# Attentions of block 2: TensorE's step takes the values of four steps back ahead of the turning of two steps back

## The chip, the cores and the metric

The kernel runs on one core of one Trainium2 chip. The metric is the device time of one execution in microseconds, median of several runs. The core's engines are named as the profile names them: PE (TensorE, matmuls), PEld (its weight loads), DVE (VectorE), ACT (ScalarE), POOL (GpSimd), SP (the engine that issues most DMAs).

## The reference

Two transformer blocks of depth 2 follow one another on 512 positions of width 1024, all in float32. The change touches only the two attentions of the second block.

```python
def attend(q, k, v, bias=None, mask=None, sink=None):
    s = jnp.einsum('...qngd,...knd->...ngqk', q, k).astype(jnp.float32) * (HEAD_DIM ** -0.5)
    if bias is not None:
        s = s + bias.astype(jnp.float32)
    if mask is not None:
        s = jnp.where(mask, s, NEG_INF)
...
    p = jax.nn.softmax(s, axis=-1)
...
    return jnp.einsum('...ngqk,...knd->...qngd', p.astype(v.dtype), v)
```

Layer 0 is a neighbourhood attention: 16 heads of 64; the 512 positions are an 8 by 64 grid, a block of 16 grid columns (128 queries) sees a window of 32 grid columns (256 keys) and all 256 context keys, with a learned bias and a mask on the window. The 256 context positions attend to the context keys alone. Layer 1 is a sliding-window attention: 16 query heads on 4 key heads, a block of 128 queries sees the positions within 128 of it and the 256 context keys, with one sink logit for each head in the softmax.

## The kernel before

Activations lie transposed in SBUF (features on the 128 partitions), so a tile of 128 features holds two heads of 64, one in each half of the partitions. Every engine has a program of its own, written out by hand in the order in which it runs; semaphores alone tie them together. No scheduler moves anything.

Both attentions are software pipelines over steps. A step `s` is one block of 128 queries of one tile (two heads). In the neighbourhood attention (`na`) a tile has 6 steps, `j, b = divmod(s, 6)`: b = 0 to 3 are the four latent blocks (scores 512 wide), b = 4 and 5 the two context blocks (256 wide); 8 tiles give 48 steps. In the sliding-window attention (`swa`) a tile has 4 steps, `tile, b = divmod(s, 4)`: b = 0 and 3 are 512 wide, b = 1 and 2 are 640 wide; 8 tiles give 32 steps. One step's data passes these stations:

- PE `score(s)` (L984 in `na`, L1068 in `swa`): queries times keys for the two heads into PSUM. `na` has two sets of PSUM banks for it and waits for the bias of two steps back; `swa` has one and waits for the bias of the step before.
- DVE `bias(s)` (L1926, L1988): adds the bias or band, with the row's minimum on the side, and writes `n_s` or `s_s` in SBUF (three buffers).
- ACT `exp(s)` (L1431, L1471): exponential with row sums, in place.
- DVE `probs(s)` (L1932 and L1935, L1995 and L1998): reciprocal and scaling. DVE runs `bias(s)` and then `probs(s-1)` in its step s.
- PE `turn(s)` (L1005, L1082): transposes the probabilities, 128 by 128 at a time, into PSUM banks of which there is one set. It waits for `probs(s)` and for `keep(s-1)`.
- ACT `keep(s)` (L1440, L1479): copies the turned probabilities to `n_pT` or `s_pT` in SBUF (two buffers). It waits for `values(s-2)`. ACT runs `exp(s)` and then `keep(s-2)` in its step s.
- PE `values(s)` (L1023, L1094): turned probabilities times values, into bank 2 or 3 of PSUM. It waits for `keep(s)`.
- DVE `take_latent`, `take_context` (L1940, L1945) and `take_out` (L2003): copy a finished tile's result out. The first `values` of a later tile waits for them.

`turn_v` (L996) is 9 extra transposes for each tile of `na`, which turn the values of the next tile; they stand at the end of the PE steps with b = 4, 5 and 0, and ACT copies them (`keep_v`, L1424). POOL builds the bias tables of the next tile of `na` meanwhile (L557), from strips that SP fetches.

In the kernel before, step s of PE is `score(s)`, `turn(s-2)`, `values(s-3)`, `turn_v`.

Of the kernel before, what the change touches and what calls it, by code (L numbers as in the profile page):

```python
# [228 lines left out]
def build(nc, d, out):  # L229
# [3 lines left out]
    with ExitStack() as stack:  # L233
# [141 lines left out]
        def bank(i, n=512):  # L375
            return ps[:, 512 * i:512 * i + n]
# [264 lines left out]
        def _(pe):  # L641
# [327 lines left out]
            def na(ph):  # L969

                def score(s):
                    j, b = divmod(s, 6)
                    if s >= 2:
                        pe.wait_ge(n_biased, 2 * (s - 1))
                    last = [None, None]
                    if b < 4:
                        window = slice(KEY_COL[b] * ROWS, KEY_COL[b] * ROWS + 2 * P)
                        parts = ((slice(b * P, b * P + P), window, 0), (slice(b * P, b * P + P), slice(S, T2), 2 * P))
                    else:
                        parts = ((slice(S + (b - 4) * P, S + (b - 3) * P), slice(S, T2), 0),)  # L980
                    for queries, keys, to in parts:
                        for hd in range(2):
                            half = slice(HD * hd, HD * hd + HD)
                            last[hd] = pe.matmul(bank(4 + 2 * (s % 2) + hd)[:, to:to + 2 * P], proj[half, j, queries],  # L984
                                                 proj[half, 8 + j, keys], start=True, stop=True)
                    for hd in range(2):
                        last[hd].then_inc(n_scored, 1)

                def turn_v(j, part):
                    if part:  # L990
                        pe.wait_ge(n_v_kept, 3 * j + part)
                    elif j >= 2:
                        pe.wait_ge(n_taken, 2 * (j - 1))
                    for t in range(4 * part, min(4 * part + 4, 9)):
                        frm = 8 * ROWS * t if t < 7 else S + (t - 7) * P
                        last = pe.transpose(bank(3)[:, t % 4 * P:t % 4 * P + P], proj[:, 16 + j, frm:frm + P], mat(IDENT))  # L996
                    last.then_inc(n_v_turned, 1)

                def turn(s):
                    pe.wait_ge(n_probs, 2 * s + 2)  # L1000
                    if s:
                        pe.wait_ge(n_kept, s)
                    for hd in range(2):
                        for c in range(4 if s % 6 < 4 else 2):
                            last = pe.transpose(bank(hd)[:, c * P:c * P + P], n_s[s % 3][:, hd, c * P:c * P + P],  # L1005
                                                mat(IDENT))
                    last.then_inc(n_turned, 1)

                def values(s):
                    j, b = divmod(s, 6)  # L1010
                    pe.wait_ge(n_kept, s + 1)
                    if b == 0:
                        pe.wait_ge(n_v_kept, 3 * j + 3)
                    if b == 4 and j < 7:
                        pe.wait_ge(n_v_kept, 3 * j + 6)
                    if j and b in (0, 4):
                        pe.wait_ge(n_taken, 2 * j - (b == 0))
                    to, tiles = (bank(2)[:, b * P:b * P + P], [KEY_COL[b] // 8, KEY_COL[b] // 8 + 2, 7, 8]) if b < 4 else \
                        (bank(3)[:, (b - 4) * P:(b - 3) * P], [7, 8])
                    for c, v in enumerate(tiles):  # L1020
                        for hd in range(2):
                            half = slice(HD * hd, HD * hd + HD)
                            last = pe.matmul(to[half, :], n_vs[j % 2][:, v, half], n_pT[s % 2][:, hd, c * P:c * P + P],  # L1023
                                             start=(c == 0), stop=(c == len(tiles) - 1))
                            if c == len(tiles) - 1:
                                last.then_inc(n_values, 1)

                pe.wait_ge(acc_free, ph["unit0"])
                for s in range(48 + 3):
                    j, b = divmod(s, 6)  # L1030
                    if s < 48:
                        score(s)
                    if j == 0 and b < 3:
                        turn_v(0, b)
                    if 2 <= s < 50:
                        turn(s - 2)
                    if s >= 3:
                        values(s - 3)
                    if s >= 4 and (s - 4) % 6 < 3 and (s + 2) // 6 < 8:
                        turn_v((s + 2) // 6, (s - 4) % 6)  # L1040

            def swa(ph):
                pe.wait_ge(acc_free, ph["unit0"])
                pe.wait_ge(hn_out, ph["hn0"])
                for n in range(len(ROPE_AT), ROPE_TILES):
                    rotate(ph, n)
                    kv = n - len(ROPE_AT)
                    if kv < 2:
                        for t in range(6):
                            last = pe.transpose(ps[:, 2 * S * kv + t * P:2 * S * kv + t * P + P],  # L1050
                                                proj[:, 10 + kv, t * P:t * P + P], mat(IDENT))
                        last.then_inc(s_v_turned, 1)
                pe.wait_ge(rope_a, ROPE_TILES)
                pe.wait_ge(rope_out, ROPE_TILES)

                def score(s):
                    tile, b = divmod(s, 4)
                    if s:
                        pe.wait_ge(s_biased, 2 * s)
                    lo, hi = max(b - 1, 0) * P, min(b + 2, 4) * P  # L1060
                    n = hi - lo
                    parts = ((lo, hi, 0), (S, T2, n)) if n == 2 * P else \
                        ((lo, hi, 0), (S, S + P, n), (S + P, T2, n + P))
                    last = [None, None]
                    for frm, end, to in parts:
                        for hd in range(2):
                            half = slice(HD * hd, HD * hd + HD)
                            last[hd] = pe.matmul(sums[hd][:, to:to + end - frm], proj[half, tile, b * P:b * P + P],  # L1068
                                                 proj[half, 8 + tile // 4, frm:end], start=True, stop=True)
                    for hd in range(2):  # L1070
                        last[hd].then_inc(s_scored, 1)

                def turn(s):
                    pe.wait_ge(s_probs, 2 * s + 2)
                    if s:
                        pe.wait_ge(s_kept, s)
                    else:
                        pe.wait_ge(s_v_kept, 2)
                    for hd in range(2):
                        for c in range(5 if 0 < s % 4 < 3 else 4):  # L1080
                            at_ = (5 * hd + c) * P
                            last = pe.transpose(ps[:, at_:at_ + P], s_s[s % 3][:, hd, c * P:c * P + P], mat(IDENT))  # L1082
                    last.then_inc(s_turned, 1)

                def values(s):
                    tile, b = divmod(s, 4)
                    pe.wait_ge(s_kept, s + 1)
                    if tile and b == 0:
                        pe.wait_ge(s_taken, tile)
                    tiles = list(range(max(b - 1, 0), min(b + 2, 4))) + [4, 5]  # L1090
                    for c, v in enumerate(tiles):
                        for hd in range(2):
                            half = slice(HD * hd, HD * hd + HD)
                            last = pe.matmul(bank(3)[half, b * P:b * P + P], s_vs[tile // 4][:, v, half],  # L1094
                                             s_pT[s % 2][:, hd, c * P:c * P + P],
                                             start=(c == 0), stop=(c == len(tiles) - 1))
                            if c == len(tiles) - 1:
                                last.then_inc(s_values, 1)

                for s in range(32 + 3):  # L1100
                    if s < 32:
                        score(s)
                    if 2 <= s < 34:
                        turn(s - 2)
                    if s >= 3:
                        values(s - 3)

            pe.wait_ge(mats_in, 16)
            for ph in phases:
# [1075 lines left out]
```

## Time and profile before

| | us |
|---|---|
| median of 3 runs | 3113.66 (3112.57 to 3115.39) |
| profiled execution, its time | 3117.72 |
| profiled execution, its span | 3115.9 |
| of it, neighbourhood attention | about 1637 to 1796 |
| of it, sliding-window attention | about 2560 to 2690 |
| PE busy over the span | 3005.2 (96%) |
| DVE, ACT, POOL busy over the span | 1598.7, 1147.8, 1093.1 |
| mean granted TensorE clock | 0.983 |

PE bounds the whole kernel, and most of it is one matmul behind the other in the projections. The two attentions together are 290 us of the span; in them PE waits for DVE and ACT at many steps, and these waits are short. The table of shares doesn't show that: the stages have to be opened one by one.

### The profile page before, as it was taken

To read this page: it belongs to the slowest core of one execution; us is meant where nothing else is said; L and a number is where in the kernel's file an instruction comes from. 1 tells how busy PE (TensorE), PEld (TensorE's weight loads), DVE (VectorE), ACT (ScalarE), POOL (GpSimd) and SP (SyncE) were. 2 spreads that over 40 slices of the span, in tenths; PEclk is the share of its full clock that TensorE was granted. 3 is DMA by queue.
4 is the path that set the end of the run, shared out by engine and by line. 5 is a ranking of instruction groups with operands and counts; after the bars stand their busy time and mean duration, and the time that the engine had idled before them with its cause. 6 is when DMAs were issued, how large, how long until landed. Compare 5 with 4: busy or idle time off the path is not lost.

```text
span 3115.9 us, 46695 instructions
## 1 busy us (share of the span) xinstructions
PE 3005.2 (96%) x16904; PEld 2405.0 (77%) x16904; DVE 1598.7 (51%) x2539; ACT 1147.8 (37%) x1756; POOL 1093.1 (35%) x506
## 2 busy tenths in 40 slices
PE   8999999999999999999998999999999999999999
PEld 6866788876857788877786678888888667778887
DVE  4457654555357554554317746541553347567272
ACT  3364442222264542232217733321232227533232
POOL 3433444443433444442232132222223330244443
PEclk9999999998999999999999999999999899999999
DMA  4421343442411343431110011121111110022223
GB/s 162 138 103 40 124 153 123 142 140 89 162 59 61 128 141 129 148 115 48 57 54 27 25 48 54 61 69 54 66 66 63 61 55 1 33 83 98 91 94 101
DMA packets 72795, 269.97 MB, mean 87 GB/s; under 512 B 7920, under 2 KB 8944, under 8 KB 72560
## 3 DMA queue, kind: packets, MB, share of 16 engines
q1 hardware_dynamic: 71024, 264.34, 25.4%
q10 hardware_dynamic: 1664, 4.18, 0.4%
q8 instruction: 70, 1.15, 0.2%
q14 instruction: 37, 0.30, 0.0%
HBM read 266.39 MB, written 2.10 MB: 86 GB/s over the span
## 4 chain that ended last, share of the span: by engine, by line
PE 56%; issue 27%; POOL 8%; DVE 6%; ACT 2%; DMA 1%; POOLq 0%; ACTq 0%; SPq 0%; DVEq 0%
PE ps L665 42%; POOL w_lo L542 7%; PE ps L692 4%; PE ps L738 1%; DVE s_s L1998 1%; PE ps L838 1%; PE ps L849 1%; PE ps L1005 1%; PE ps L1023 1%; PE ps L984 1%; DVE s_s L1988 1%; PE ps L873 1%; PE ps L830 1%; DVE n_s L1935 1%; DMA w_raw<-w_in_dram 1%
## 5 line engine op out<-in xcount | busy, mean ns | idle before, releaser
L542 POOL TENSOR_TENSOR w_lo<-w_raw,w_hi 128x1024 fp32r<-128x1024 f32 (+1 forms) x364 | 945.7, 2599 | 1526.0 <-ACT w_hi L1142 1526.0
L665 PE MATMUL ps<-h_hi,w_hi 128*128 128x512 f32 (+1 forms) x2832 | 957.7, 372 | 3.4 <-POOL w_lo L542 1.7
L665 PE MATMUL ps<-h_lo,w_hi 128*128 128x512 f32 (+1 forms) x2832 | 946.8, 368 | 0.0
L665 PE MATMUL ps<-h_hi,w_lo 128*128 128x512 f32 (+1 forms) x2832 | 945.4, 368 | 0.0
L1142 ACT ACTIVATE w_hi<-w_raw 128x1024 fp32r<-128x1024 f32 (+1 forms) x364 | 406.4, 1117 | 1369.0 <-PE ps L665 1219.1
L665 PEld LDWEIGHTS ps<-h_hi,w_hi 128*128 128x128 f32 x2832 | 491.2, 188 | 109.4 <-issue 7.3
L665 PEld LDWEIGHTS ps<-h_lo,w_hi 128*128 128x128 f32 x2832 | 491.9, 188 | 90.1
L665 PEld LDWEIGHTS ps<-h_hi,w_lo 128*128 128x128 f32 x2832 | 490.5, 188 | 91.7
L1778 DVE TENSOR_SCALAR conv_y<-u_pad,small 128x770 f32<-128x770 f32 (+1 forms) x88 | 175.8, 1997 | 196.1 <-ACT u_pad L1323 195.6
L1576 DVE CUSTOM_DVE_ANT_0 mod_junk<-mod_w,silu_c 128x1024 f32<-128x1024 f32 x96 | 138.4, 1442 | 127.1 <-DMA mod_w<-w_mod_dram 126.5
L1731 DVE SCALAR_TENSOR_TENSOR xT<-ps,mod,xT 128x512 f32 (+1 forms) x72 | 45.5, 659 | 304.4 <-PE ps L665 259.0
L1781 DVE SCALAR_TENSOR_TENSOR conv_y<-u_pad,small,conv_y 128x770 f32<-128x770 f32 (+1 forms) x176 | 156.1, 887 | 24.4 <-DVE conv_y L1781 6.7
L1579 DVE CUSTOM_DVE_ANT_0 mod_junk<-mod_w,silu_c 128x1024 f32<-128x1024 f32 x96 | 152.9, 1593 | 3.3
L1755 DVE TENSOR_TENSOR glu_a<-ps,glu_g 128x512 f32<-128x512 f32 x44 | 30.5, 692 | 188.6 <-PE ps L665 181.9
L1757 DVE TENSOR_TENSOR b_lo<-glu_a,b_hi 128x512 f32 x44 | 105.5, 2397 | 41.6 <-ACT b_hi L1304 41.6
L665 PE MATMUL ps<-a_hi,w_hi 128*128 128x512 f32 (+1 forms) x396 | 119.9, 357 | 1.5 <-POOL w_lo L542 1.5
L665 PE MATMUL ps<-a_lo,w_hi 128*128 128x512 f32 (+1 forms) x396 | 120.0, 357 | 0.0
L665 PE MATMUL ps<-a_hi,w_lo 128*128 128x512 f32 (+1 forms) x396 | 120.0, 357 | 0.0
L665 PE MATMUL ps<-b_hi,w_hi 128*128 128x512 f32 x264 | 104.8, 397 | 2.8 <-POOL w_lo L542 2.8
L665 PE MATMUL ps<-b_hi,w_lo 128*128 128x512 f32 x264 | 104.4, 395 | 0.0
L665 PE MATMUL ps<-b_lo,w_hi 128*128 128x512 f32 x264 | 104.4, 395 | 0.0
L1731 DVE SCALAR_TENSOR_TENSOR xT<-ps,xT 128x512 f32 (+1 forms) x48 | 33.2, 691 | 130.9 <-PE ps L665 104.9
(212 smaller groups left out, 3792.7 us busy)
## 6 DMA issues: line engine op xcount, KB each, us to landing
mod_w<-w_mod_dram SPq DMA_DIRECT2D x96, 512.0 KB, 3.4
w_raw<-w_gu_dram SPq DMA_DIRECT2D x88, 512.0 KB, 3.3
w_raw<-w_down_dram SPq DMA_DIRECT2D x64, 704.0 KB, 4.0
w_raw<-w_up_dram SPq DMA_DIRECT2D x88, 512.0 KB, 3.3
w_raw<-w_in_dram SPq DMA_DIRECT2D x56, 512.0 KB, 3.4
w_raw<-na_qkv_dram SPq DMA_DIRECT2D x24, 512.0 KB, 3.2
w_raw<-w_out_dram SPq DMA_DIRECT2D x16, 512.0 KB, 3.3
w_raw<-swa_qkv_dram SPq DMA_DIRECT2D x12, 512.0 KB, 3.3
```

Of the source, the lines that this page charges most:

```text
L542: pool.tensor_tensor(w_lo[par][:, 0:cols], w_raw[par][:, 0:cols], w_hi[par][:, 0:cols].bitcast(F32), ALU.subtract).then_inc(w_lo_ready, 1)
L665: last = pe.matmul(acc[par][:, to:to + n], w[par][:, k * P:k * P + P], r[:, k, frm:frm + n], start=begin, stop=end)
L692: last = pe.matmul(acc[par][:, to:to + n], w[par][:, k * P:k * P + P], r[:, k, frm:frm + n], start=begin, stop=end)
L738: return [pe.matmul(sums[0][:, to:to + w], mats[g // 2 * HD:g // 2 * HD + HD, SPREAD64 + g % 2, :], r[g // 2 * HD:g // 2 * HD + HD, frm:fr ...
L830: pe.matmul(bank(hd), proj1[half, 12 + j, b * P:b * P + P], proj1[half, 8 + j, :], start=True, stop=True).then_inc(x_scored, 1)
L1142: act.activation(w_hi[par][:, 0:K * P], w_raw[par][:, 0:K * P], ACT.Copy).then_inc(w_hi_ready, 1)
L1576: dve.tensor_tensor_reduce(mod_junk[:], mod_w[:], silu_c[:, 0, :], 1.0, 0.0, ALU.mult, ALU.add, mod_sum[:, 0:1]).then_inc(mod_step, 1)
L1579: dve.tensor_tensor_reduce(mod_junk[:], mod_w[:], silu_c[:, 1, :], 1.0, 0.0, ALU.mult, ALU.add, mod_sum[:, 1:2]).then_inc(mod_step, 1)
L1731: last = dve.scalar_tensor_tensor(out=x_, in0=row(acc[par][:, to:to + n]), scalar=gate, in1=x_, op0=ALU.mult, op1=ALU.add)
L1757: dve.tensor_tensor(b_lo[:, bass.ds(f, 1), :], row(glu_a[:]), b_hi[:, bass.ds(f, 1), :].bitcast(F32), ALU.subtract).then_inc(a_lo_ready, 1)
L1778: dve.tensor_scalar(y, u, tap(0), tap(3), ALU.mult, ALU.add).then_inc(conv_step, 1)
L1781: dve.scalar_tensor_tensor(out=y, in0=u, scalar=tap(j), in1=y, op0=ALU.mult, op1=ALU.add).then_inc(conv_step, 1)
```

## The change

In both attentions PE's step s becomes `score(s)`, `values(s-4)`, `turn(s-2)`, `turn_v`: the values come ahead of the turning, and they are those of one step further back. The loop has one more step to finish. No instruction is added or taken away (PE has the same number of instructions), and the programs of DVE, ACT, POOL and SP are the same as before, as are all buffers and all waits.

```diff
@@ na @@
-                for s in range(48 + 3):
+                for s in range(48 + 4):
                     j, b = divmod(s, 6)
                     if s < 48:
                         score(s)
                     if j == 0 and b < 3:
                         turn_v(0, b)
+                    if s >= 4:
+                        values(s - 4)
                     if 2 <= s < 50:
                         turn(s - 2)
-                    if s >= 3:
-                        values(s - 3)
                     if s >= 4 and (s - 4) % 6 < 3 and (s + 2) // 6 < 8:
                         turn_v((s + 2) // 6, (s - 4) % 6)
@@ swa @@
-                for s in range(32 + 3):
+                for s in range(32 + 4):
                     if s < 32:
                         score(s)
+                    if s >= 4:
+                        values(s - 4)
                     if 2 <= s < 34:
                         turn(s - 2)
-                    if s >= 3:
-                        values(s - 3)
```

On PE in the neighbourhood attention, the end of step b = 4, step b = 5 and step b = 0 of a tile. `n_s_132` to `n_s_134` are the three buffers of probabilities (L1005 is `turn`), `n_pT_135` and `n_pT_136` the two of turned probabilities (L1023 is `values`), `proj_77` in L984 is `score` and in L996 `turn_v`. Before:

```order
L1005 MATMUL ps<-mats_59,n_s_134 128x128 x8
L1023 MATMUL ps<-n_pT_136,n_vs_130 64x128 x8
L996 MATMUL ps<-mats_59,proj_77 128x128 x4
L984 MATMUL ps<-proj_77 128x256 x2
L1005 MATMUL ps<-mats_59,n_s_132 128x128 x8
L1023 MATMUL ps<-n_pT_135,n_vs_130 64x128 x8
L996 MATMUL ps<-mats_59,proj_77 128x128 x4
L984 MATMUL ps<-proj_77 128x256 x4
```

The same place in the changed kernel:

```order
L1005 MATMUL ps<-mats_59,n_s_134 128x128 x8
L996 MATMUL ps<-mats_59,proj_77 128x128 x4
L984 MATMUL ps<-proj_77 128x256 x2
L1023 MATMUL ps<-n_pT_136,n_vs_130 64x128 x8
L1005 MATMUL ps<-mats_59,n_s_132 128x128 x8
L996 MATMUL ps<-mats_59,proj_77 128x128 x4
L984 MATMUL ps<-proj_77 128x256 x4
L1023 MATMUL ps<-n_pT_135,n_vs_130 64x128 x8
```

The values that stood between a turning and the next score now stand behind that score.

On PE in the sliding-window attention, from the turning in a step b = 2 on; `s_s` are probabilities (L1082), `s_pT` turned ones (L1094), L1068 is `score`. Before:

```order
L1082 MATMUL ps<-mats_59,s_s_142 128x128 x8
L1094 MATMUL ps<-s_pT_145,s_vs_140 64x128 x10
L1068 MATMUL ps<-proj_77 128x384 x2
L1068 MATMUL ps<-proj_77 128x128 x4
L1082 MATMUL ps<-mats_59,s_s_143 128x128 x8
L1094 MATMUL ps<-s_pT_146,s_vs_140 64x128 x8
L1068 MATMUL ps<-proj_77 128x256 x4
```

The same place in the changed kernel:

```order
L1082 MATMUL ps<-mats_59,s_s_142 128x128 x8
L1068 MATMUL ps<-proj_77 128x384 x2
L1068 MATMUL ps<-proj_77 128x128 x4
L1094 MATMUL ps<-s_pT_145,s_vs_140 64x128 x10
L1082 MATMUL ps<-mats_59,s_s_143 128x128 x8
L1068 MATMUL ps<-proj_77 128x256 x4
L1094 MATMUL ps<-s_pT_146,s_vs_140 64x128 x8
```

Here too a turning is followed directly by the next score, and each group of values stands between that score and the next turning.

## Rows read from the trace of the kernel before

**Rows 1.** Windows of the two stages: length, busy PE, PEld, DVE, ACT, POOL; clock.

```profile
1636.00:1797.00 161.00, 142.10 (x1352) 102.79 (x1352) 119.78 (x400) 117.77 (x271) 34.82 (x44) 1.00 0.08 25
2531.00:2692.00 161.00, 141.67 (x1305) 107.96 (x1304) 112.89 (x320) 93.71 (x173) 17.57 (x13) 0.96 0.04 13
```

**Rows 2.** Waits in the neighbourhood attention: us in total, times, longest.

```profile
PEld ps L1023 <- issue: 7.9, 47, 0.2
PE ps L1005 <- DVE n_s L1935: 11.7, 26, 0.7
...
DVE pace L1922 <- issue: 17.5, 9, 2.3
DVE n_s L1926 <- issue: 14.2, 9, 1.8
```

**Rows 3.** Waits of PE in the sliding-window attention, window 2575 to 2682.

```profile
PE ps L1082 <- ACT s_pT L1479: 4.5, 14, 0.4
PE ps L1094 <- DVE proj L2003: 4.0, 7, 0.6
```

**Rows 4.** Timeline, neighbourhood attention, steps b = 4, 5, 0: start, duration, what, [idle before].

```profile
1688.97 1.09 PE L1005 MATMUL ps<-mats,n_s 128*128 128x128 f32 x8 [0.44 <-DVE n_s L1935]
...
1689.99 1.09 PE L1023 MATMUL ps<-n_pT,n_vs 128*64 128x128 f32 x16
...
1691.02 0.66 PE L996 MATMUL ps<-mats,proj 128*128 128x128 f32 x4
1691.60 0.70 PE L984 MATMUL ps<-proj 64*128 64x256 f32 x4
...
1692.24 1.09 PE L1005 MATMUL ps<-mats,n_s 128*128 128x128 f32 x8
1692.39 0.42 DVE L1926 CUSTOM_DVE_ANT_0 n_s<-ps,n_bias 128x256 f32<-128x256 f32 x1 [1.78 <-issue]
...
1694.87 1.13 PE L984 MATMUL ps<-proj 64*128 64x256 f32 x8
...
1696.16 0.06 DVE L1922 MEMSET pace<- 128x1 f32 x1 [2.27 <-issue]
```

**Rows 5.** The same timeline at the next step b = 4.

```profile
1707.35 1.00 ACT L1440 ACTIVATE n_pT<-ps 128x1024 f32<-128x1024 f32 x1
...
1708.38 0.41 DVE L1926 CUSTOM_DVE_ANT_0 n_s<-ps,n_bias 128x256 f32<-128x256 f32 x1
...
1708.51 1.09 PE L1005 MATMUL ps<-mats,n_s 128*128 128x128 f32 x8 [0.44 <-DVE n_s L1935]
```

**Rows 6.** Timeline, sliding-window attention, one tile from b = 3 to b = 3.

```profile
2603.61 0.75 DVE L1988 CUSTOM_DVE_ANT_0 s_s<-ps,s_band,small 128x512 f32<-128x512 f32 x1 [0.49 <-issue]
...
2603.93 1.28 PE L1082 MATMUL ps<-mats,s_s 128*128 128x128 f32 x10 [0.40 <-ACT s_pT L1479]
...
2605.78 1.09 PE L1094 MATMUL ps<-s_pT,s_vs 128*64 128x128 f32 x16 [0.57 <-DVE proj L2003]
...
2606.81 1.13 PE L1068 MATMUL ps<-proj 64*128 64x256 f32 x8
2607.87 1.31 PE L1082 MATMUL ps<-mats,s_s 128*128 128x128 f32 x10
...
2609.11 1.31 PE L1094 MATMUL ps<-s_pT,s_vs 128*64 128x128 f32 x20
...
2610.36 1.36 PE L1068 MATMUL ps<-proj 64*128 64x384 f32 x12
...
2611.80 0.88 DVE L1988 CUSTOM_DVE_ANT_0 s_s<-ps,s_band,small 128x640 f32<-128x640 f32 x1 [1.27 <-issue]
...
2614.36 1.00 ACT L1479 ACTIVATE s_pT<-ps 128x1024 f32<-128x1024 f32 x1
...
2615.50 1.07 PE L1082 MATMUL ps<-mats,s_s 128*128 128x128 f32 x8 [0.23 <-ACT s_pT L1479]
...
2618.74 0.75 DVE L1988 CUSTOM_DVE_ANT_0 s_s<-ps,s_band,small 128x512 f32<-128x512 f32 x1 [0.49 <-issue]
```

## The prediction, made before the changed kernel was run

> **What bounds the kernel now.** I read the windows of the two stages first: PE is busy 142 of 161 us in each, DVE 120 and 113, ACT 118 and 94 [rows 1]. So PE is the fullest engine, but in neither stage full, and what it could gain there is at most its gaps. The granted clock is 1.00 (the 2.4 GHz level) in the first window and 0.96 in the second, which takes in the slow start of that stage; nothing in the steady steps is explained by the clock. Next come the waits. In the neighbourhood attention PE waits 26 times in front of a turning for DVE's scaling, and DVE is idle in two places only, 9 times each, for 31.7 us in all: about once in every tile in front of the bias of step b = 5 and once in front of that of b = 0 [rows 2]. In the sliding-window attention PE waits in front of turnings for ACT's copy of turned probabilities and, once in a tile, in front of the values for the taking of the tile before [rows 3]. Last the timelines of one tile of each, which give a chain that closes on itself.
>
> **How a tile of the neighbourhood attention runs.** The time from the start of one PE group to the start of the next is what the group costs PE. Read as differences of starts: a turning of 8 transposes costs 1.02 (1688.97 to 1689.99), the values 1.03, a `turn_v` of four 0.58, a narrow score 0.64, the turning, values and `turn_v` of step 5 together 2.63, a wide score 1.06 (the wide one is taken from the sliding-window stage, 2606.81 to 2607.87) [rows 4, 6]. DVE's bias starts 0.15 behind the end of a narrow score, and about 0.23 behind that of a wide one; the turning of step 4 starts 0.13 behind DVE's start of that step. From step b = 0 to the next b = 4 DVE never waits: it goes from 1696.16 to 1708.38, 12.22 us without a wait [rows 4, 5], which the two idle places of rows 2 confirm. So the tile's cycle is: 0.13, then on PE turning 1.02, values 1.03, `turn_v` 0.58, score 0.64, turning 1.02, values 1.03, `turn_v` 0.58, score 1.06, then 0.23 and DVE's 12.22. The sum is 19.54; the trace has 1708.51 - 1688.97 = 19.54 [rows 4, 5]. PE sets the time from b = 4 to b = 0, DVE the rest.
>
> **Part 1, the neighbourhood attention.** In the new order the values of step 4 stand ahead of the turning that waits 0.44 for DVE. They are ready, since their copy was waited for by an earlier turning. Of the cycle above one of the two groups of values, 1.03, drops out: behind DVE's release PE goes turning, `turn_v`, score, (values, turning), `turn_v`, score. The second group stays, as PE is behind there and has no wait to put it in. For this the values must be done before DVE releases the turning of step 4. They are: between the turning of step b = 3 and that of b = 4 PE has the same three groups in either order (turning, values, narrow score), and in the old one they are done in time for a wait of 0.44 [rows 4, 5]. ACT's copy in front of it ends at 1708.35, 0.16 ahead of the turning at 1708.51 [rows 5], and hangs on DVE, not on the values. The new cycle is 18.5 us, 1.03 less, in 8 tiles: 8.2 us. The last tile has no `turn_v` and no POOL beside it; its chain of turnings, values and score is the same, so I take the same term there.
>
> What is late next: DVE from b = 0 to b = 4, so that moving the values in those steps brings nothing; only 1 of 6 steps pays. Nothing is added to a queue: SP's fetches and POOL's tables hang on DVE's bias and come 1 us earlier each tile with it.
>
> **Part 2, the sliding-window attention.** A tile takes 2618.74 - 2603.61 = 15.13 us [rows 6]. PE's groups, as differences of starts: scores 1.06 (b = 0, 3) and 1.29 (b = 1, 2: 2610.36 to the bias at 2611.80, less 0.15); turnings 1.24 (x10: b = 1, 2) and 1.02 (x8); values 1.03 (x16: b = 0, 3) and 1.25 (x20: b = 1, 2) [rows 4, 6]. Twice each: 4.70 + 4.52 + 4.56 = 13.78. The difference, 1.35, is PE's waits: 0.40 and 0.23 for ACT's copies, 0.57 for the taking, each with the short hole that the sequence leaves around it [rows 6].
>
> In the new order each of the three is covered. (a) ACT's copy in step b = 1 ends at 2615.36, 3.56 behind that step's bias at 2611.80, and the next turning can start 3.70 behind it [rows 6]. With values of 1.03 or 1.25 between score and turning, PE reaches it at turning + score + values = 3.3 to 3.8 behind the turning before, and walking through the four steps of a tile PE arrives 0.5 to 1.1 us after the copy. (b) The first values of a tile now stand in the next step, about 1.0 us behind the end of the taking. (c) The single score buffer is the new risk, since a score now comes directly behind a turning. The bias of b = 2 starts 0.15 behind its score's end; PE has values 1.25 and a turning 1.02 to do and reaches score b = 3 at 2.12 behind the bias's start. The bias is two passes of 0.88, and with 0.1 for the passing on it is over after about 1.8. That leaves 0.3, the tightest place. So PE should not wait at all, and the tile takes 13.78: 1.35 less. Between the bias of the first b = 3 and that of the last lie 7 tiles: 9.5 us. The first steps run at the lower clock and have no values yet, and the last turnings and values hang on ACT's copies one by one, so the ends get nothing (0 to 0.5).
>
> **The unknown cost, the new neighbours.** A group of values directly behind a score occurs nowhere in the trace; before, all values follow a turning. From rows: 16 values cost 1.03 and 8 turnings 1.02 whatever follows, a score of the same work 1.06, so a follower of a score costs 0.04 more than one of another group [rows 4, 6]. I take 0: one group follows a score in either order. Bounds: the loader idles 0.17 in front of nearly every group of values [rows 2]; if that hole vanishes or doubles behind a score, the sliding-window stage changes by 32 x 0.17 = 5.4 us and the PE part of the other (2 of 6 steps, 16 in all) by 2.7, together 8.1 us either way.
>
> The Trainium skill ("TensorE: Matmul & The Clock Gate", section "Step-by-step: what each phase is for") says that a weight load runs ahead of matmuls in flight when its row group doesn't conflict or it goes to the background buffer. By its first condition the loads of the values (all rows) conflict with a score (half the rows) as those of a turning do, and the sum stays 17.7; by its second the hole of 0.17 should not be there at all, and the gain could be up to the 8.1 us larger. The loader's wait in rows 2, 47 times, speaks for the first.
>
> **Sum.** 8.2 + 9.5 = 17.7 us. The profiled execution would go from 3117.7 to 3100.0; it lies 4.1 above the median of the runs, and that difference stays. For the median: 3113.7 - 17.7 = 3096.0.
>
> **Rivals.**
> (1) *Only one stage gains.* In the neighbourhood stage it may be that ACT's copy, which is only 0.16 ahead of the turning now, holds it; then 3113.7 - 9.5 = 3104.2. In the other the score buffer or the copy may take the place of the waits, since each margin there is under half a microsecond at its tightest; then 3105.5. For it: the margins. Against: the chains above reproduce the old cycle to 0.02 us.
> (2) *The waits only move.* PE waits in front of the turning for as long as before plus the values' time, and the gain is gone: 3113.7. For it: DVE sets 4 of 6 steps. Against: DVE idles 31.7 us in the stage [rows 2], and it idles for PE.
> (3) *Slower: the turning is what is urgent.* In the steps where PE is behind (b = 5, 0, 1 of each tile, 24 in all) the turning starts one group of values later. ACT's copy follows it, and the next exponential stands behind that copy in ACT's queue. If this chain were critical it would cost 24 x 1.03 = 24.7 against 17.7: 3120.7. It decides from where the copy ends later than the next bias's first half; a turning 1.02, a copy 1.00 and two passings of about 0.1 make 2.2 us, and the next turning comes 2.9 us or more later. So 0.7 us is left, and the trace speaks against it.
> (4) *More gain*, by the loads of the values pulled under the score: 3096.0 - 8.1 = 3087.9.
> That the change doesn't do what it says can be left out: the order on PE shows it.
>
> **Chances.** Forecast 0.68 (own range 3092 to 3100, small errors of neighbours and ends), rival 1 0.14, rival 2 0.08, rival 3 0.04, rival 4 0.06. From 3091 to 3107 lie the forecast and rival 1, with a part of rival 4: above 8 in 10. Faster by over 0.2% (6.2 us, about what a measurement can tell from no change) are the forecast and rivals 1 and 4: 0.88. Same 0.08, slower 0.04.
>
> **What the profile of the changed kernel would show.** A tile of the neighbourhood attention from turning to turning in 18.5 instead of 19.54; DVE's idle time in front of b = 5 falls from 1.78 to about 0.75, that in front of b = 0 stays at 2.3. The sliding-window tile in 13.8 instead of 15.1, with no wait for L2003 and none for L1479 in the steady tiles. It would be wrong if PE's values behind a score start later than 0.2 us behind the score's other followers, if DVE or ACT waits appear in front of L984 or L1068, or if the cycle stays at 19.5 or 15.1.

## The result, and the profile after

The changed kernel takes 3098.44 us, the median of 4 runs (3094.91 to 3103.38), against 3114.52 for the kernel before (4 runs, 3112.57 to 3119.8). The ratio is 0.9947, with a 95% interval of 0.9931 to 0.9963. Measured again beside the experiments it took 3096.06 (6 runs, 3094.19 to 3098.2) against 3113.85, ratio 0.9943 (0.9931 to 0.9955). So it is faster by 16 to 18 us; 17.7, and a median of 3096.0, had been forecast.

First the windows of the two stages, to set beside [rows 1]. Columns: start and end, length, busy PE, PEld, DVE, ACT, POOL, clock, DMA share, GB/s. After:

```profile
1638.40:1787.10 148.70, 138.38 (x1352) 102.84 (x1352) 119.73 (x400) 114.43 (x267) 34.82 (x43) 1.00 0.09 27
2557.10:2681.10 124.00, 117.78 (x1188) 92.43 (x1189) 94.54 (x299) 90.82 (x170) 5.02 (x5) 0.94 0.02 6
```

The same two stretches, cut at like places, in the kernel before:

```profile
1637.10:1796.10 159.00, 142.10 (x1352) 102.79 (x1352) 119.78 (x400) 115.89 (x268) 34.82 (x43) 1.00 0.08 25
2562.20:2695.40 133.20, 118.05 (x1187) 92.18 (x1188) 94.60 (x298) 90.57 (x170) 5.06 (x4) 0.95 0.02 5
```

The stages are 10.3 and 9.2 us shorter. DVE is as busy as before to a tenth of a microsecond, and PE in the second stage to 0.3: what went is idle time. In the first stage PE's busy time fell as well, by 3.7 us with the same 1352 matmuls, which the prediction had not foreseen. About 3 us of it are transposes that now stand next to transposes (see e6).

The waits of the changed kernel in the neighbourhood attention, window 1640 to 1787 (total, times, longest), answer to [rows 2]:

```profile
DVE pace L1922 <- PE ps L984: 16.0, 9, 2.1
PEld ps L1023 <- issue: 12.8, 40, 0.3
...
PE ps L1005 <- DVE n_s L1935: 5.6, 13, 0.4
...
DVE n_s L1926 <- issue: 4.3, 7, 0.6
```

DVE's wait in front of step b = 5 fell from 1.8 to 0.6, and the one in front of b = 0 is still there, 2.1 instead of 2.3. PE waits for DVE's scaling 13 times instead of 26. In the sliding-window attention no wait of PE for L1479 or L2003, the two of [rows 3], is left in the window 2570 to 2668. One wait of 0.3 us for DVE's bias stands there, in front of the score at 2570.75, where the stage comes out of the low clock.

The timeline of one tile of the neighbourhood attention, steps b = 4, 5, 0 and the next b = 4 (start, duration, what, [idle before]), answers to [rows 4, 5]:

```profile
1687.63 1.09 PE L1005 MATMUL ps<-mats,n_s 128*128 128x128 f32 x8 [0.44 <-DVE n_s L1935]
...
1688.56 0.60 PE L996 MATMUL ps<-mats,proj 128*128 128x128 f32 x4
...
1689.09 0.70 PE L984 MATMUL ps<-proj 64*128 64x256 f32 x4
1689.72 1.09 PE L1023 MATMUL ps<-n_pT,n_vs 128*64 128x128 f32 x16
...
1689.87 0.42 DVE L1926 CUSTOM_DVE_ANT_0 n_s<-ps,n_bias 128x256 f32<-128x256 f32 x1 [0.61 <-issue]
...
1690.74 1.09 PE L1005 MATMUL ps<-mats,n_s 128*128 128x128 f32 x8
...
1691.67 0.60 PE L996 MATMUL ps<-mats,proj 128*128 128x128 f32 x4
...
1692.20 1.13 PE L984 MATMUL ps<-proj 64*128 64x256 f32 x8
...
1693.50 0.06 DVE L1922 MEMSET pace<- 128x1 f32 x1 [2.13 <-PE ps L984]
...
1705.72 0.41 DVE L1926 CUSTOM_DVE_ANT_0 n_s<-ps,n_bias 128x256 f32<-128x256 f32 x1
...
1705.85 0.88 PE L1005 MATMUL ps<-mats,n_s 128*128 128x128 f32 x6 [0.44 <-DVE n_s L1935]
```

The tile takes 1705.85 - 1687.63 = 18.22 us (19.54 before, 18.5 forecast). DVE's part, 1693.50 to 1705.72, is 12.22, the very value of before. PE's part is 1693.50 - 1687.63 = 5.87. As differences of starts, turning 0.93, `turn_v` 0.53, score 0.63, values 1.02, turning 0.93, `turn_v` 0.53, and the wide score with what DVE needs behind it 1.30.

One tile of the sliding-window attention after, from b = 1 on, answers to [rows 6]:

```profile
2589.29 0.88 DVE L1988 CUSTOM_DVE_ANT_0 s_s<-ps,s_band,small 128x640 f32<-128x640 f32 x1 [1.06 <-issue]
...
2592.70 1.31 PE L1094 MATMUL ps<-s_pT,s_vs 128*64 128x128 f32 x20
2592.85 0.88 DVE L1988 CUSTOM_DVE_ANT_0 s_s<-ps,s_band,small 128x640 f32<-128x640 f32 x1 [0.79 <-issue]
...
2593.94 1.09 PE L1082 MATMUL ps<-mats,s_s 128*128 128x128 f32 x8
...
2594.97 1.13 PE L1068 MATMUL ps<-proj 64*128 64x256 f32 x8
...
2596.03 1.09 PE L1094 MATMUL ps<-s_pT,s_vs 128*64 128x128 f32 x16
...
2597.05 1.31 PE L1082 MATMUL ps<-mats,s_s 128*128 128x128 f32 x10
...
2597.52 0.69 DVE L2003 COPY proj<-ps 128x512 f32<-128x512 f32 x1
...
2598.30 1.14 PE L1068 MATMUL ps<-proj 64*128 64x256 f32 x8
...
2599.36 1.09 PE L1094 MATMUL ps<-s_pT,s_vs 128*64 128x128 f32 x16
...
2603.07 0.88 DVE L1988 CUSTOM_DVE_ANT_0 s_s<-ps,s_band,small 128x640 f32<-128x640 f32 x1 [1.05 <-issue]
```

From bias to bias 13.78 us, as forecast, and no PE row has an idle time in brackets: in these tiles PE is now the bound.

### The profile page after: what moved, and what is told of

It reads as the page before. It is cut to its first block, busy times and chain, and to the rows that moved or that the text cites. A ratio compares the mean times of both kernels' runs of the same rounds, so it can differ in the third digit from the quotient of the medians.

```text
span 3101.6 us, 46695 instructions
## 1 busy us (share of the span) xinstructions
PE 3004.8 (97%) x16904; PEld 2405.6 (78%) x16904; DVE 1600.4 (52%) x2539; ACT 1146.6 (37%) x1756; POOL 1091.8 (35%) x506
## 4 chain that ended last, share of the span: by engine, by line
PE 56%; issue 26%; POOL 8%; DVE 6%; ACT 2%; DMA 1%; POOLq 0%; ACTq 0%; SPq 0%; DVEq 0%
PE ps L665 43%; POOL w_lo L542 7%; PE ps L692 4%; PE ps L738 1%; PE ps L849 1%; DVE s_s L1998 1%; PE ps L838 1%; DVE n_s L1935 1%; DVE s_s L1988 1%; PE ps L830 1%; PE ps L1005 1%; PE ps L873 1%; PE ps L984 1%; PE ps L752 1%; PE ps L1023 1%
```

## The experiments

All kernels keep the programs of DVE, POOL and SP, and ACT's too but for one run, named there. What differs is the order on PE. The stages' lengths, from the first score's start to the end of the last values in each profile, serve to compare them, since the rest of a span moves by itself (see the last section). Stage 1 is the neighbourhood attention, stage 2 the sliding-window attention. The columns: the tile that repeats in each stage, each stage's length, the end of each stage (from DVE's bias of b = 4, or of b = 3, in the last tile to the end of the last values), and the ratio to before with its interval.

| run | tile 1 | tile 2 | stage 1 | stage 2 | end 1 | end 2 | ratio (95%) |
|---|---|---|---|---|---|---|---|
| before | 19.55 | 15.13 | 158.4 | 128.8 | 9.3 | 9.6 | |
| changed kernel | 18.24 | 13.78 | 148.2 | 119.5 | 9.4 | 9.6 | 0.9947 (0.9931 to 0.9963) |
| e1 only stage 1 | 18.25 | 15.13 | 148.2 | 129.0 | 9.4 | 9.6 | 0.9967 (0.9955 to 0.9979) |
| e2 only stage 2 | 19.55 | 13.78 | 158.4 | 119.5 | 9.3 | 9.6 | 0.9975 (0.9966 to 0.9984) |
| e3 lag alone | 20.56 | 15.49 | 168.5 | 136.4 | 12.6 | 14.7 | 1.0063 (1.0048 to 1.0079) |
| e4 order alone | 19.30 | 16.65 | 159.2 | 145.7 | 11.8 | 14.3 | 1.0064 (1.0049 to 1.0079) |
| e5 one step ahead | 19.63 | 15.13 | 161.1 | 128.8 | 11.6 | 9.6 | 1.0016 (1.0007 to 1.0026) |
| e6 `turn_v` next | 19.27 | 15.13 | 156.2 | 128.9 | 9.3 | 9.6 | 0.9991 (0.9982 to 1.0001) |
| e7 `turn_v` later | 17.93 | 13.77 | 146.7 | 119.3 | 9.3 | 9.6 | 0.9935 (0.9923 to 0.9947) |
| e8 some steps ahead | 18.75 | 14.48 | 153.9 | 127.2 | 10.9 | 12.0 | 0.9980 (0.9970 to 0.9989) |

**e1 and e2: each stage alone.** The change is made in `na` alone, then in `swa` alone.

> Only the neighbourhood attention has the new order, the sliding-window attention the old one. Theory A (one group of values, 1.03 us, leaves the chain of PE between the turning of step b = 4 and the score of b = 0; the transposes that now follow transposes switch faster by a further 0.3 us a tile): a tile takes 18.2 us as in the changed kernel, the time falls by 9 to 10 us. The sliding-window tile stays at 15.1 us. Rival B (the two attentions help each other, or part of the gain is a matter of the clock): the time falls by clearly more or less than that, and the two single gains do not add up to the whole.

> Only the sliding-window attention has the new order. Theory A (PE's waits for ACT's copy and for the taking of a finished tile are covered by values): a tile takes 13.8 us against 15.1, the time falls by 9.3 us. The tile of the neighbourhood attention stays at 19.5 us. Rival B: as for the run before, the gains do not add up.

Measured: 3103.73 and 3106.13 us against 3114.72, so -11.0 and -8.6. The stages' lengths change by -10.2 and -9.3, each as in the full change, and the other stage stays. The two parts are independent, and both are real: the medians add up to 19.6 us, the stages to 19.5. Rival 1 falls.

**e3: the longer lag without the new order.**

```diff
                     if 2 <= s < 50:
                         turn(s - 2)
-                    if s >= 3:
-                        values(s - 3)
+                    if s >= 4:
+                        values(s - 4)
```

and the same in `swa`, with the loops one step longer.

> In both attentions the values are those of four steps back, but behind the turning as in the kernel before: score(s), turn(s-2), values(s-4), turn_v. Theory A (order and lag are both needed): in the neighbourhood attention nothing changes, 19.5 us a tile. In the sliding-window attention the wait for the taking goes, but ACT's copy now waits for the values behind the turning; the loop turning, values, copy gives 3.7 us in two steps and 3.5 in the others, 14.4 us a tile, so some 5 us less for the kernel. Rival C (it is the lag alone that gives the gain): 18.2 and 13.8 us a tile, 16 us less.

Measured: 3133.65 us, 18.9 more. This missed: both stages got slower, by 1.0 and 0.4 us a tile. The trace shows whose wait it is, in step b = 1 and, below, in b = 5 (L1940 is the taking of a tile, L1440 the copy of turned probabilities, L1023 the values):

```profile
1701.19 0.69 DVE L1940 COPY proj<-ps 128x512 f32<-128x512 f32 x1 [0.58 <-PE ps L1023]
...
1711.76 1.02 ACT L1440 ACTIVATE n_pT<-ps 128x1024 f32<-128x1024 f32 x1 [0.82 <-PE ps L1023]
```

Two engines wait in it for values that now stand behind a turning. DVE's taking of a finished tile hangs on the last values of that tile, and DVE's scaling of the next probabilities is queued behind the taking. ACT's copy needs the buffer that the values of four steps back read.

The tiles are less than half of the loss: from the first tile's b = 4 or 3 to the last one's the stages lose 6.9 and 1.8 us. Another 3.3 and 5.1 are lost in the two ends, where no score stands between the last turnings, and PE, DVE and ACT wait for each other in turn. In the sliding-window attention (in the kernel before, ACT's copy at that place had waited 1.46 for its turning):

```profile
2695.09 2.21 PE L1082 MATMUL ps<-mats,s_s 128*128 128x128 f32 x10 [1.95 <-DVE s_s L1998]
...
2699.18 1.24 ACT L1479 ACTIVATE s_pT<-ps 128x1280 f32<-128x1280 f32 x1 [4.67 <-PE ps L1094]
...
2700.56 1.06 PE L1082 MATMUL ps<-mats,s_s 128*128 128x128 f32 x8 [1.52 <-ACT s_pT L1479]
```

A part of these 5.1 us is the clock: the granted clock was 0.66 from 2696 to 2700, after PE had been busy for 2.05 of the 4 us before, and the turning took 2.21 instead of 1.28. That part may differ from execution to execution.

**e4: the new order without the longer lag.** The values of three steps back stand ahead of the turning.

> In both attentions the values come ahead of the turning, but they are those of three steps back as in the kernel before: score(s), values(s-3), turn(s-2), turn_v. Theory A (the values must be ready when PE comes to them): in the neighbourhood attention a tile stays at 19.5 us, since the copy that the values wait for ends when DVE releases the turning. In the sliding-window attention PE waits for the copy and, once a tile, for the taking in front of the values, and the turning comes later by both: some 16.3 us a tile, 8 us more for the kernel. Rival D (the order alone gives the gain): 18.2 and 13.8 us a tile, 16 us less.

Measured: 3132.58 us, 17.9 more, where 8 had been expected. The neighbourhood stage changes by only 0.8 us (its tiles are 0.25 shorter, its end 2.5 longer), the sliding-window stage by 16.9. Four of its tiles take 16.65, near the 16.3 expected; what was missed are the end, 4.7 longer, and two slower tiles (below). A turn of one tile there:

```profile
2639.33 0.69 DVE L2003 COPY proj<-ps 128x512 f32<-128x512 f32 x1
...
2640.16 1.09 PE L1094 MATMUL ps<-s_pT,s_vs 128*64 128x128 f32 x16 [2.26 <-DVE proj L2003]
```

The first values of a tile stand in step b = 3, ahead of the turning, and need the bank that DVE empties in that same step, behind a bias that itself waits for that step's score. PE waits 15.8 us for it in 7 tiles. The lag of four moves those values to the next step, where the taking is over. So neither half of the change shortens a stage alone: the order needs the lag, and the lag needs the order. Here two of the tiles took 18.1 and 18.2 instead of 16.65. In both the granted clock fell for some microseconds, while the other tiles of the same program kept 1.00. The first of them, with PE busy for 3.18 and then 2.54 of 4 us:

```profile
2600.00:2604.00 4.00, 3.18 (x32) 2.40 (x32) 3.58 (x13) 2.64 (x5) 0.00 (x0) 1.00 0.00 0
2604.00:2608.00 4.00, 2.54 (x19) 2.24 (x20) 2.40 (x8) 1.52 (x4) 0.00 (x0) 0.64 0.00 0
```

**e5: values ahead of the turning in step b = 4 alone**, in `na`, behind it in all others, with the lag of four. The prediction had said that only this step pays.

```diff
+                    if s >= 4 and b == 4:
+                        values(s - 4)
                     if 2 <= s < 50:
                         turn(s - 2)
-                    if s >= 3:
-                        values(s - 3)
+                    if s >= 4 and b != 4:
+                        values(s - 4)
```

> Only the neighbourhood attention is changed: values of four steps back in all steps, but ahead of the turning in step b = 4 alone; in the five others they stand behind it as before. Theory A (only b = 4 pays, since DVE sets the pace from b = 0 to b = 4 and PE is behind in b = 5): a tile takes 18.4 us (the full change has 18.2; one of the two cheap switches from turning to the turning of values is lost), 9 us less for the kernel. Rival G (every step's wait gives a share): a tile takes about 19.3 us, a sixth of the gain.

Measured: 3118.14 us against 3113.85, the tile 19.63, the end of the stage 2.3 longer. Missed by 1.2 us a tile. Step b = 4 does what was said (DVE's idle time in front of the bias of b = 5 is 0.61, as in the full change, and the tile is 0.93 shorter than in e3), but the other steps give it back:

```profile
1706.48 0.42 DVE L1947 COPY proj<-ps 128x256 f32<-128x256 f32 x1 [0.58 <-PE ps L1023]
...
1710.60 1.07 PE L1005 MATMUL ps<-mats,n_s 128*128 128x128 f32 x8 [0.32 <-ACT n_pT L1442]
```

**e8: values ahead where a taking hangs on them.** To tell the takings (theory T) from ACT's copies (theory C), the values stand ahead in steps b = 1, 3 and 4 of the neighbourhood attention and in step b = 3 of the other, behind in the rest.

```diff
@@ na, against e5 @@
-                    if s >= 4 and b == 4:
+                    if s >= 4 and b in (1, 3, 4):
                         values(s - 4)
                     if 2 <= s < 50:
                         turn(s - 2)
-                    if s >= 4 and b != 4:
+                    if s >= 4 and b not in (1, 3, 4):
                         values(s - 4)
@@ swa, against the kernel before @@
+                    if s >= 4 and s % 4 == 3:
+                        values(s - 4)
                     if 2 <= s < 34:
                         turn(s - 2)
-                    if s >= 3:
-                        values(s - 3)
+                    if s >= 4 and s % 4 != 3:
+                        values(s - 4)
```

> The values are those of four steps back everywhere, but they stand ahead of the turning only where a taking by DVE or the b = 4 turning hangs on them: in steps b = 1, 3 and 4 of the neighbourhood attention, and in step b = 3 of the sliding-window attention. In all other steps they stand behind the turning. Theory T (the longer lag costs what it does because DVE's takings of a finished tile, which stand ahead of DVE's scalings, wait for values behind a turning): the neighbourhood tile of 19.63 us with values ahead in b = 4 alone loses the two takings' waits of 0.58 and comes to 18.5; the sliding-window tile of 15.49 us with all values behind loses the 1.28 that the taking waited, 14.2. The whole: 8 x 1.04 + 7 x 0.93 = 14.8 us less than before, about 3099. Theory C (what costs is that ACT's copies wait for values that stand behind the turning; the takings' waits are cover for that): the copies still wait in the steps left, so the neighbourhood tile stays at 19.2 or more and the sliding-window tile at 15.1 or more; about 3112 or longer.

Measured: tiles of 18.75 and 14.48, 3109.18 us against 3115.95. The takings bring 0.88 of the 1.16 expected (from e5's 19.63) and 1.01 of the 1.28 (from e3's 15.49), below theory C's floors of 19.2 and 15.1. In the neighbourhood attention only the takings' waits went: ACT's copies wait for values 7 times and 6.3 us in the window 1650 to 1780 of e5 as of e8, and the takings, 13 times and 7.3 us in e5, no longer. There the takings are shown to be the cause. In the sliding-window attention the copy of step b = 3 waited for the same values as the taking (0.45 beside 1.28 in e3), so the run moves both; that the next turning waited 0.88 in e3 for DVE's scaling, which is queued behind the taking, speaks for the taking.

0.5 and 0.7 us are left to the full change's 18.24 and 13.78. PE's waits for copies in the steady tiles of e8, windows 1650 to 1780 and 2570 to 2665:

```profile
PE ps L1005 <- ACT n_pT L1444: 2.5, 8, 0.3
...
PE ps L1084 <- ACT s_pT L1483: 3.7, 13, 0.4
```

In the neighbourhood tile this wait makes 0.39 of the 0.51: score and wait in step b = 5 take 1.02, the score 0.63 in the full change. The other 0.12 come from the turning and `turn_v` of that step, which don't stand side by side (e6). In the other tile two such waits, each with its short hole, make the 0.7.

The whole got 6.1 us shorter by its stages and 6.8 by the medians, less than half of the 14.8 expected: the tiles gave 6.1 and 4.3, and the ends, where the values stand behind the turning, took back 1.6 and 2.5.

**e6: what a neighbour costs.** In the old order, `turn_v` stands between the turning and the values, in `na`.

```diff
                         turn(s - 2)
-                    if s >= 3:
-                        values(s - 3)
                     if s >= 4 and (s - 4) % 6 < 3 and (s + 2) // 6 < 8:
                         turn_v((s + 2) // 6, (s - 4) % 6)
+                    if s >= 3:
+                        values(s - 3)
```

> Only the neighbourhood attention is changed, and neither lag nor order of values and turning: the turning of values (turn_v) stands directly behind the turning and ahead of the values of three steps back. Theory A (the surplus of 0.3 us a tile over the forecast is a faster switch between two groups of transposes, 0.93 against 1.02 us for the group in front): a tile takes 19.3 to 19.4 us against 19.54, 1 to 2 us less for the kernel. Rival H (the surplus has to do with the values' new place): 19.5 us a tile, no change.

Measured: the tile 19.27, and on PE:

```profile
1685.68 1.09 PE L1005 MATMUL ps<-mats,n_s 128*128 128x128 f32 x8 [0.46 <-DVE n_s L1935]
1686.61 0.60 PE L996 MATMUL ps<-mats,proj 128*128 128x128 f32 x4
1687.14 1.09 PE L1023 MATMUL ps<-n_pT,n_vs 128*64 128x128 f32 x16
1688.16 0.70 PE L984 MATMUL ps<-proj 64*128 64x256 f32 x4
1688.79 1.09 PE L1005 MATMUL ps<-mats,n_s 128*128 128x128 f32 x8
```

Turning 0.93 and `turn_v` 0.53, where they cost 1.02 and 0.58 in [rows 4]; the values keep 1.02. Only the two groups of transposes that stand side by side got cheaper, the one in front by 0.09 and the one behind by 0.05. The ratio, 0.9991 (0.9982 to 1.0001), can't be told from no change; the tile can.

**e7: `turn_v` and ACT's copy of it one step later**, on top of the full change. In step b = 4 the score then follows the turning directly.

```diff
-                    if s >= 4 and (s - 4) % 6 < 3 and (s + 2) // 6 < 8:
-                        turn_v((s + 2) // 6, (s - 4) % 6)
+                    if s >= 5 and (s - 5) % 6 < 3 and (s + 1) // 6 < 8:
+                        turn_v((s + 1) // 6, (s - 5) % 6)
```

and the same condition for `keep_v` on ACT.

> The changed kernel with turn_v, and ACT's copies of it, one step later: at the end of the steps b = 5, 0 and 1 in place of 4, 5 and 0. Theory A (the chain of PE from the turning of b = 4 to the score of b = 0 is what a tile is waiting for, and it holds two groups of turn_v): one of them, 0.5 to 0.6 us, leaves the chain and goes where PE waits for DVE; a tile takes 17.7 us against 18.2, some 4 us less than the changed kernel, 20 less than the one before. Rival I (something else is late by then, as ACT's copies): 18.2 us a tile as in the changed kernel.

Measured: 3093.54 us (3091.97 to 3095.29) against 3096.06 for the changed kernel beside it, 2.5 less where 4 had been expected. The two ranges overlap a little; the stage is 1.5 shorter. It is the fastest version here. DVE's idle time in front of b = 5 falls again, as the same mechanism says:

```profile
1701.99 0.42 DVE L1926 CUSTOM_DVE_ANT_0 n_s<-ps,n_bias 128x256 f32<-128x256 f32 x1 [0.17 <-issue]
...
1711.77 0.66 PE L1023 MATMUL ps<-n_pT,n_vs 128*64 128x128 f32 x8 [0.41 <-ACT n_pT L1440]
```

The tile is 17.93, not 17.7, for two reasons. With no transposes behind it the turning of b = 4 costs 1.02 again, so PE's part from there to DVE's start of b = 0 is 5.44 against 5.87, 0.43 less and not 0.53. And step b = 1 now holds a full `turn_v` instead of a short one, so PE is the pace from b = 0 to b = 1 (turning, `turn_v`, score and values, 3.11 us together): from DVE's bias of b = 0 to that of b = 1 it is 3.11 instead of 2.99.

**The changed kernel again**, for the unchanged stretches.

> The changed kernel once more, unaltered, to have a second profile of it on another occasion. Both theories on the tiles: 18.22 and 13.78 us a tile again, to 0.05. Theory E (the 1.3 to 4 us by which unchanged stretches differ between the first two profiles are the moments at which the granted clock rises and falls, which differ from execution to execution): the stretches between landmarks outside the attentions differ again by 1 us or more from the first profile, and with them the total. Rival F (the new order itself makes PE find a lower clock at the start of the projection behind the neighbourhood attention, 0.77 and 0.89 in the first 10 us of it against 1.00 before): the same low values stand there again.

Measured: the attentions take 148.2 and 119.3, as in the first profile to 0.2, and its span is 3092.8 instead of 3101.6. Behind the last tile of the neighbourhood attention the first profile had a low clock, this one the full one:

```profile
1788.00:1793.00 5.00, 4.01 (x15) 3.30 (x16) 4.26 (x2) 5.00 (x7) 4.95 (x3) 0.77 0.00 0
1793.00:1798.00 5.00, 5.00 (x27) 4.29 (x27) 5.00 (x3) 1.61 (x3) 4.40 (x2) 0.89 0.00 0
```

and the second profile at that place:

```profile
1785.00:1790.00 5.00, 3.90 (x19) 2.96 (x20) 4.29 (x2) 5.00 (x7) 4.98 (x3) 1.00 0.00 0
1790.00:1795.00 5.00, 5.00 (x30) 4.35 (x29) 5.00 (x3) 1.58 (x3) 4.39 (x2) 1.00 0.00 0
```

So the low clock there is one execution's, not the change's. Over the whole spans the mean granted clock is 0.983 in the first profile and 0.986 in the second.

## Why the prediction was right

**The mechanism of part 1 held, its size was under-estimated.** DVE's chain of 12.22 us stayed to the hundredth, and the wait in front of b = 5 fell to 0.61 (0.75 forecast). The tile lost 1.31 instead of 1.03. The mis-sized term is the sum of PE's groups: the rows of before gave a turning 1.02 and a `turn_v` 0.58, because values stood between them. In the new order the two stand side by side, and they cost 0.93 and 0.53. Twice (0.09 + 0.05) = 0.28 is the whole surplus. e6 confirms it with another order. The term "8 x 1.03 = 8.2" has two more errors that nearly cancel: 6 tiles repeat, not 8, and the last one gained 2.50 (19.23 to 16.73), not 1.03. Together 6 x 1.31 + 2.50 = 10.4, against 10.2 measured by the stage.

**Why the last tile gains more.** The prediction took "the same term" for a tile without POOL beside it. Without POOL, DVE is no longer the pace there. DVE's scaling (L1935) in one step of a steady tile of the changed kernel, and in the like step of the last tile:

```profile
1700.77 1.84 DVE L1935 TENSOR_SCALAR n_s<-n_s,stats 128x512 f32<-128x512 f32 x2
...
1773.50 0.88 DVE L1935 TENSOR_SCALAR n_s<-n_s,stats 128x512 f32<-128x512 f32 x2
```

While POOL builds its tables the scaling takes 1.51 to 1.84, else 0.88. From b = 0 to b = 4 DVE needs 12.22 in a steady tile of either kernel; in the last tile it took 11.90 before (1774.36 to 1786.26) and takes 10.74 after (1766.43 to 1777.17), and these 1.16 are nearly all of what the last tile gains beyond 1.31. There the loop through PE and ACT sets the pace of several steps, and the values drop out of it more than once: in the kernel before, the bias of b = 2 started at 1780.16 and that of b = 3 at 1783.24, 3.08 apart, with PE's turning waiting 0.42 for ACT's copy; after, 1772.08 and 1774.61, 2.53 apart. The Trainium skill ("Perfetto Trace Analysis", section "Optimizing Scalar/DVE Operations") says that GpSimd and DVE share an SBUF read port; the trace fits that, with 1.84 against 0.88.

**"Only 1 of 6 steps pays"** held in the steady tiles as to what the order gains over the old one, and fails as a recipe: e5 shows that the other steps need the new order too, to pay for the longer lag. The prediction priced the lag at nothing. That was right only because the order comes with it, and it had not said so. e3 puts the price of the lag alone at 18.9 us, of which 8.7 lie in the tiles and 8.4 in the ends of the stages, in part at a low clock; in the full change the ends are as before to 0.2.

**Part 2 held in every step.** 13.78 was forecast and measured. The margins: (a) the copy of b = 1 ends at 2592.86, the turning starts at 2593.94, 1.08 behind it; (b) the taking ends at 2598.21, the values start at 2599.36; (c) the tight one, the second bias of b = 2 ends at 2594.54 (2593.66 + 0.88) and the next score starts at 2594.97, 0.43 behind it, where 0.3 was forecast. Seven tiles by 1.35 are 9.5; the stage lost 9.3.

**The new neighbour cost nothing**, as taken. A narrow score followed by values costs 0.63 (0.64 before), a wide one 1.06 (2594.97 to 2596.03). The loader's hole in front of the values is what changed, from 0.2 at most to 0.3, in 40 places; the matmuls' starts don't show it. The bound had been made from that hole, and it was not a cost at all. So rival 4 and the second condition of the page cited there ("TensorE: Matmul & The Clock Gate" of the Trainium skill, section "Step-by-step: what each phase is for") get no support: the hole didn't vanish, it grew, and the values' price stayed.

**The sum.** The stages gave 10.2 + 9.3 = 19.5, against 17.7. By medians it was 16.1 the first time and 17.8 the second. The 1.8 of surplus lies within what the unchanged stretches vary by, so that a median falls on the forecast to 0.1 is luck; what was right is each part and its size to within 2 us. Rival 2 (the waits only move) falls with DVE's idle time of b = 5, rival 3 (the turning is urgent) with the tiles: its margin of 0.7 us sufficed. The waits that it is built from exist, though, once the values stand on the wrong side of the turning, as e3 shows for ACT's copy.

## What to carry to other kernels

Put the work that nobody waits for in front of the instruction that waits, and check both of its ends: what frees its inputs, and which engine is queued behind something that needs its output. A lag and an order that are each a loss alone can be a gain together, so undo them one at a time before judging either. Read a group's cost as the difference of starts for the neighbour that it will have, since the same eight transposes cost 1.02 or 0.93 by what follows. Look at the ends of the stages too: in four of these runs a few microseconds were lost there that no steady tile shows.

## What the runs showed of the hardware

- Eight transposes of 128 x 128 (f32) cost 1.02 us when values or a score follow and 0.93 when four more transposes do. Those four cost 0.53 behind the eight, whether values or a score follow them, and 0.58 behind values or a score. Sixteen matmuls of values cost 1.02 to 1.03 whatever stands around them.
- DVE's scaling of 2 x 128x512 takes 0.88 us, and 1.51 to 1.84 while POOL adds its tables.
- In stretches whose program is the same, executions differ. From the end of the last values of the neighbourhood attention to the first score of the sliding-window attention it took 759.7 to 768.5 us in eleven profiles, and 768.5 and 763.4 in two of one kernel. Between these two the clock differs (0.77 and 0.89 against 1.00 over 10 us, above). For the eleven it isn't the whole cause: e1, with the highest mean clock (0.988), took 764.9, and e5, with 0.986, 759.7. Differences of a few microseconds must be read from stages, not from one span.
